# Delta rule on one core: transposed keys in another PSUM bank, scratch of level 0 in a third, output sums one projection step later

## The chip, the cores and the metric

The kernel runs on one core of one Trainium2 chip. The metric is the device time of one execution in microseconds, given as the median of three runs. One further execution was taken with the hardware profiler; all rows below come from it.

## The reference

The reference is a two-layer encoder trunk over 512 tokens of width 1024. Layer 1 has, beside a memory attention, a gated delta rule with 8 heads of width 128. That part is what matters here:

```python
m = where(strict, einsum('bhncd,bhnsd->bhncs', k_beta, k) * decay, 0)
t_inv = triangular_solve(eye + m, eye, lower=True, unit_diagonal=True)
u = t_inv @ v_beta
w = t_inv @ (k_beta * exp(g))
k_dec = k * exp(g_last - g)
def step(state, inp):                 # chunk after chunk
    v_new = u_c - w_c @ state
    o     = qd @ state + a_c @ v_new
    state = state * gl + k_dec^T @ v_new
    return state, o
o = rms_norm(o, out_norm) * silu(z)   # per head, before the output projection
```

The kernel computes it in chunks of 128 tokens, four to a head (`NT = 4`), and inverts `eye + m` level by level: level 0 on single elements, levels 1 to 4 inside 32x32 blocks, level 5 joins 32 to 64, level 6 joins 64 to 128.

## The kernel before

Everything is written out by hand per engine: five instruction streams, each in its own order, held together by semaphores. No planner moves anything. `wait_ge(S.x, n)` holds that engine's whole stream until semaphore `x` has counted to `n`.

Projections are made with fp32 split into two rounded parts, so each 128x128 weight tile costs three matmuls of 512 columns (`product`, L622). A head needs four weight blocks of eight such tiles: queries, keys, values, gate z. These 32 tiles of the **next** head are dealt out between the small matmuls of the delta rule of this head: `fill(first, end)` issues the tiles of that range, and one tile is called a dense portion here. So TensorE has projection work to do while VectorE and ScalarE prepare the next small operand.

The order on TensorE in `delta(h)` (L753) around the change is: two dense portions; the row of decays and betas of the head, broadcast by one matmul (L764) into bank `D[2]`; four transposes of the normalised keys `KN` (L634, from `transposes4`) into `D[5]`; one portion; the Gram matrix of the keys (L772) into `D[1]`; the sums over the squared outputs of the **previous** head (`output_sums`, L730 and L731) into `D[0]`; six portions (3 to 9); the products of keys and queries (L782) into `D[0]`; three portions; then the levels, each with two groups of small matmuls (L797 and L820 for levels 1 to 4, L801, L823 and L827 for level 5, L805 and L830 for level 6). At level 5 a part goes into `D[5]`. The four chunks of the recurrence follow (L845 to L865), which add up the head's output in `D[5]`. The group L797 writes `D[3]`.

`D[5]` therefore holds the outputs of the previous head until VectorE has read them in `o_t1` (L1963, recorded at L1709, inside `stt`). That is why the key transposes wait for `o_t1`.

VectorE's order over the border between two heads is: `normed_k` (the keys times their inverse norm, at L1703, counts `kn_done`), the sum of squares of the outputs (L1960), a copy of the projected z (L1712), `o_t1` (L1709), the decay mask (L1878, reads `D[2]`), `split_o` (L1706, counts `osq_lo`, on which `output_sums` waits), a copy of the values (L1712), the Gram matrix times decays (L1703, after `gg_done` and ScalarE's `dm_done`), level 0 (four quarter multiplies into `D[3]`, a subtraction, and `V.transpose` at L1893, which counts `y_done`), `o_finish` (L1867, after ScalarE's `o_rstd`), and `kdec` (L1897: the transposed keys in PSUM times decays, counts `kdec_done`). The convolution taps of the next head and the levels come behind it.

ScalarE's order is: the exponential of the decay row from `D[2]`, the squares of q, four exponentials of the decay mask (L1427), `o_root` (logarithm and exponential over the output sums, after `oss`), the copy `MM` of the Gram matrix (after `z_pre`, counts `t_done`), then rounding the next weight block (`upper`) and the first tap of the convolution (L1358), and so on.

All elementwise helpers record their own line, so many different instructions share L1248 (ScalarE) and L1703, L1706, L1709, L1712 (VectorE).

Of the kernel before, what the change touches and what calls it, by code (L numbers as in the profile page):

```python
# [23 lines left out]
P = 128  # L24
# [65 lines left out]
QB = P // 4  # L90
(IDENT, ONES, ONES64, TRIU, NEG_LOWER, SMALL) = range(6)
SMALL_IDENT, SMALL_LEVEL0 = 0, 1
# [34 lines left out]
def yoco_kernel(nc, x, mem, w_stream, w_out, w_down, w_ba, cols_in, squares_in, dist_in, out):  # L127
    with ExitStack() as ctx:
# [21 lines left out]
        bank = ctx.enter_context(nc.psum_tensor("bank", [P, 8, 512], F32))  # L150
# [164 lines left out]
        def due(n):  # L315

            return not isinstance(n, int) or n > 0
# [16 lines left out]
        def w(i):  # L334
            return ws[:, i, :]

        def w4(i):
            return ws[:, i, :].rearrange("p (t c) -> p t c", t=NT)

        def sq(i):  # L340
            return sq_c[:, i, :]

        def small(i):

            at = SMALL * P + QB * i
            flat = sq_c[:].rearrange("p a c -> p (a c)")[:, at:at + QB]
            return flat.unsqueeze(1).to_broadcast([P, NT, QB])

        def half_rows(q):
            return slice(HB * q, HB * (q + 1))  # L350

        def quarter(q):
            return slice(QB * q, QB * (q + 1))

        def per_tile(ap):
            return ap.rearrange("p (t c) -> p t c", t=NT)

        def key_block(t, q, c):

            return ws[quarter(q), MM, P * t + QB * c:P * t + QB * (c + 1)]  # L360

        def inverse(t, q):

            return ws[quarter(q), TT, QB * t:QB * (t + 1)]

        def turned(t, q):

            return ws[quarter(q), TT, P + QB * t:P + QB * (t + 1)]

        def masked(t, q):  # L370

            return ws[quarter(q), PM, QB * t:QB * (t + 1)]

        def upper_half(t):

            return ws[half_rows(0), TT, 2 * P + HB * t:2 * P + HB * (t + 1)]
# [12 lines left out]
        def psum(b, n=512):  # L389
            return bank[:, b, 0:n]  # L390

        def psum4(b):
            return bank[:, b, :].rearrange("p (t c) -> p t c", t=NT)

        def tt(i, t):
            return ws[:, i, t * P:(t + 1) * P]
# [4 lines left out]
        D = [2, 3, 4, 5, 6, 7]  # L401
# [11 lines left out]
        NG, GG, _, GL, EDEC, LNB, TMP1, TMP2 = range(8)  # L413

        def dn(i):
            return dn_s[:, i, :].rearrange("p (h t) -> p h t", h=DN_HEADS)

        def dn_bcast(i, h):

            return dn(i)[:, h, :].unsqueeze(2).to_broadcast([P, NT, P])  # L420
# [192 lines left out]
        def _(pe):  # L613
# [18 lines left out]
            def transposes4(dst, source):  # L632
                for t in range(NT):
                    mm = nc.tensor.transpose(bank[:, dst, t * P:(t + 1) * P], tt(source, t), sq(IDENT))  # L634
                return mm
# [105 lines left out]
            def output_sums(h):  # L741

                pe.wait_ge(S.osq_lo, h + 1)
                two_part_sums(D[0], act_lo[:, OHI_T, :], act_lo[:, OLO_T, :]).then_inc(S.oss, 1)
# [8 lines left out]
            def delta(h, fill):  # L753
# [9 lines left out]
                    pe.wait_ge(S.v_done, NT * h)  # L763
                nc.tensor.matmul(psum(D[2]), pick(h), gate_rows, start=True, stop=True).then_inc(S.gb_done, 1)  # L764
                pe.wait_ge(S.kn_done, h + 1)
                if due(h):
                    pe.wait_ge(S.o_t1, h)
                transposes4(D[5], KN).then_inc(S.ktr_done, 1)
                fill(2, 3)

                for t in range(NT):
                    mm = nc.tensor.matmul(bank[:, D[1], t * P:(t + 1) * P], tt(KN, t), tt(KN, t), start=True, stop=True)  # L772
                mm.then_inc(S.gg_done, 1)
                if due(h):
                    output_sums(h - 1)
                fill(3, 9)

                pe.wait_ge(S.c_ready, 2 * h + 1)
                if due(h):
# [5 lines left out]
                for k in range(1, LEVELS):  # L785
                    quarters, join, last = k < LEVELS - 2, k == LEVELS - 2, k == LEVELS - 1
                    if k == 1:
                        pe.wait_ge(S.t_done, h + 1)
                        pe.wait_ge(S.y_done, Y_PER_HEAD * h + 1)
                    else:  # L790
                        pe.wait_ge(S.tz_done, TZ_PER_HEAD * h + k - 1)
                    if last:
                        pe.wait_ge(S.y_done, Y_PER_HEAD * h + LEVELS)
                    for t in range(NT):
                        if quarters:
                            for q in range(4):
                                mm = nc.tensor.matmul(bank[quarter(q), D[3], QB * t:QB * (t + 1)],  # L797
                                                      key_block(t, q, q), inverse(t, q), start=True, stop=True)
                        elif join:
                            for r in range(2):  # L800
                                mm = nc.tensor.matmul(bank[quarter(2 * r + 1), D[3], QB * t:QB * (t + 1)],  # L801
                                                      key_block(t, 2 * r, 2 * r + 1), inverse(t, 2 * r),
                                                      start=True, stop=True)
                        else:
                            mm = nc.tensor.matmul(bank[half_rows(1), D[3], HB * t:HB * (t + 1)],  # L805
                                                  ws[half_rows(0), MM, P * t + HB:P * (t + 1)], upper_half(t),
                                                  start=True, stop=True)
                    mm.then_inc(S.p_mm, 1)
                    fill(10 + 2 * k, 11 + 2 * k)
                    pe.wait_ge(S.p_done, P_PER_HEAD * h + (k if quarters else LEVELS - 1 if join else LEVELS))  # L810
                    pe.wait_ge(S.y_done, Y_PER_HEAD * h + (Y_PER_HEAD - 2 if last else k))
                    if k == 1:
                        pe.wait_ge(S.vb_done, h + 1)
                        pe.wait_ge(S.kdec_done, h + 1)
                    if last:
                        pe.wait_ge(S.tz_done, TZ_PER_HEAD * h + LEVELS - 1)
                    for t in range(NT):
                        if quarters:
                            for q in range(4):
                                mm = nc.tensor.matmul(bank[quarter(q), D[4], QB * t:QB * (t + 1)], turned(t, q),  # L820
                                                      masked(t, q), start=True, stop=True)
                        elif join:
                            nc.tensor.matmul(bank[quarter(1), D[5], QB * t:QB * (t + 1)], turned(t, 1), masked(t, 1),  # L823
                                             start=True, stop=True)
                            for r in range(2):
                                q = 2 * r + 1
                                mm = nc.tensor.matmul(bank[quarter(2 * r), D[4], QB * t:QB * (t + 1)], masked(t, q),  # L827
                                                      turned(t, q), start=True, stop=True)
                        else:
                            mm = nc.tensor.matmul(bank[half_rows(0), D[2], HB * t:HB * (t + 1)],  # L830
                                                  ws[half_rows(1), PM, HB * t:HB * (t + 1)],
                                                  ws[half_rows(1), ZZ, P * t + HB:P * (t + 1)], start=True, stop=True)
                    mm.then_inc(S.tz_mm, 1)
                    fill(11 + 2 * k, 12 + 2 * k)
# [65 lines left out]
            def next_heads(h):  # L900

                def fill(first, end):
                    for j in range(first // KT, (end - 1) // KT + 1):
                        proj_dn(h + 1, j, range(max(first - KT * j, 0), min(end - KT * j, KT)))
                return fill
            each_head(lambda h: delta(h, next_heads(h)))

            def mem_project(layer, j, ks):
# [790 lines left out]
        def _(dve):  # L1699
            V = nc.vector  # L1700

            def mul(out_, x_, y_):
                return V.tensor_tensor(out_, x_, y_, ALU.mult)  # L1703

            def sub(out_, x_, y_):
                return V.tensor_tensor(out_, x_, y_, ALU.subtract)  # L1706
# [169 lines left out]
            def delta(h, fill, following=True):  # L1876
# [8 lines left out]
                mul(psum(D[1]), psum(D[1]), w(DD)).then_inc(S.mt_done, 1)  # L1885
                dve.wait_ge(S.mt_done, h + 1)
                for q in range(4):
                    mul(per_tile(bank[quarter(q), D[3], 0:P]), psum4(D[1])[quarter(q), :, QB * q:QB * (q + 1)],
                        small(SMALL_LEVEL0)[quarter(q)]).then_inc(S.z_pre, 1)
                dve.wait_ge(S.z_pre, 4 * h + 4)  # L1890
                sub(per_tile(w(TT)[:, P:2 * P]), small(SMALL_IDENT), per_tile(psum(D[3], P))).then_inc(S.z_done, 1)
                dve.wait_ge(S.z_done, h + 1)
                V.transpose(w(TT)[:, 0:P], w(TT)[:, P:2 * P]).then_inc(S.y_done, 1)  # L1893
                if due(h):
                    o_finish(h - 1)
                dve.wait_ge(S.ktr_done, h + 1)
                mul(w4(KDEC), psum4(D[5]), dn_bcast(EDEC, h)).then_inc(S.kdec_done, 1)  # L1897
                fill(0, 1)
                for k in range(1, LEVELS):
                    n = (LEVELS - 1) * h + k  # L1900
# [345 lines left out]
```

## Time and profile before

| | |
|---|---|
| median of three runs | 1453.14 us (1451.79 to 1453.53) |
| profiled execution, its own time | 1453.59 us |
| profiled execution, span | 1451.8 us |
| TensorE matmul busy | 1411.7 us, 97% of the span |
| VectorE / ScalarE / GpSimd busy | 546.5 / 576.8 / 560.4 us |
| mean granted TensorE clock | 0.995 of full speed |

The span runs from the first to the last instruction; the time of an execution is some 1.8 us more. Starts are in us from the start of the span. A matmul row's duration is modelled from start to drain and successive matmuls overlap, so distances between starts tell what a matmul costs the stream. An entry in square brackets is idle time of that engine before the row, and what released it.

### The profile page before, as it was taken

How to read it: one execution, taken by the hardware profiler on the slowest of the kernel's cores; microseconds unless marked ns; L12 is line 12 of the kernel's file. 1: busy time of each engine (PE TensorE's matmuls, PEld its weight loads, DVE VectorE, ACT ScalarE, POOL GpSimd, SP SyncE). 2: the span in 40 equal slices, each digit the busy share in tenths (PEclk: the TensorE clock that was granted, in tenths of full speed). 3: DMA queues.
4: the chain of work that ended last, by engine and by line, in shares of the span. 5: the costliest groups of instructions: out<-in, count | busy, mean ns of one | idle time of the engine just before them, and what ended most of it. 6: DMA issues, size and time to landing. Idle time of an engine off the chain costs nothing.

```text
span 1451.8 us, 24193 instructions
## 1 busy us (share of the span) xinstructions
PE 1411.7 (97%) x9320; PEld 1137.8 (78%) x9320; DVE 546.5 (38%) x1052; ACT 576.8 (40%) x985; POOL 560.4 (39%) x276
## 2 busy tenths in 40 slices
PE   5999999999999999999999999999999999999998
PEld 5977777777777888888888887778788888888887
DVE  3545666666644222210122224774322221122210
ACT  5654544554525342322223334875334232223221
POOL 3543233333321444354434443122345344433432
PEclk9999999999999999999999999999999999999999
DMA  6431111111110423233332242111233323422232
GB/s 237 131 105 55 60 59 59 46 57 40 47 54 26 125 93 109 85 91 108 101 101 79 80 125 91 48 49 45 77 109 102 102 69 100 135 84 91 74 95 78
DMA packets 39230, 124.15 MB, mean 86 GB/s; under 512 B 4192, under 2 KB 5472, under 8 KB 39136
## 3 DMA queue, kind: packets, MB, share of 16 engines
q1 hardware_dynamic: 38976, 122.55, 27.1%
q8 instruction: 69, 1.13, 0.3%
q10 hardware_dynamic: 160, 0.26, 0.1%
q14 instruction: 25, 0.20, 0.0%
HBM read 120.44 MB, written 2.10 MB: 84 GB/s over the span
## 4 chain that ended last, share of the span: by engine, by line
PE 90%; DVE 5%; ACT 3%; issue 1%; DMA 0%; DVEq 0%; SPq 0%; ACTq 0%
PE bank L622 78%; DVE ws L1709 2%; ACT ws L1248 1%; PE bank L945 1%; PE bank L820 1%; PE bank L973 1%; DVE ws L1712 1%; ACT L1450 1%; DVE act_lo L1709 1%; PE bank L797 1%; PE bank L1180 1%; PE bank L1204 1%; PE bank L1191 1%; PE bank L962 0%; PE bank L772 0%
## 5 line engine op out<-in xcount | busy, mean ns | idle before, releaser
L558 POOL TENSOR_TENSOR w_lo<-w_raw,w_hi 128x1024 fp32r<-128x1024 f32 (+1 forms) x248 | 529.4, 2150 | 771.2 <-ACT w_hi L1248 771.2
L622 PE MATMUL bank<-act_hi,w_hi 128*128 128x512 f32 (+1 forms) x1776 | 709.6, 400 | 4.0 <-DVE act_lo L1709 2.6
L622 PE MATMUL bank<-act_hi,w_lo 128*128 128x512 f32 (+1 forms) x1776 | 680.0, 383 | 0.0
L622 PE MATMUL bank<-act_lo,w_hi 128*128 128x512 f32 (+1 forms) x1776 | 679.6, 383 | 0.0
L622 PEld LDWEIGHTS bank<-act_hi,w_hi 128*128 128x128 f32 x1776 | 335.0, 189 | 71.1 <-issue 4.9
L622 PEld LDWEIGHTS bank<-act_hi,w_lo 128*128 128x128 f32 x1776 | 334.7, 188 | 65.8
L622 PEld LDWEIGHTS bank<-act_lo,w_hi 128*128 128x128 f32 x1776 | 335.5, 189 | 58.6 <-issue 3.1
L1248 ACT ACTIVATE w_hi<-w_raw 128x1024 fp32r<-128x1024 f32 (+1 forms) x248 | 228.6, 952 | 93.1 <-PE bank L622 91.0
L1703 DVE TENSOR_TENSOR ws<-bank,ws 128x512 f32<-128x512 f32 x110 | 75.9, 691 | 334.5 <-PE bank L622 324.3
L1248 ACT ACTIVATE ws<-ws 128x512 f32<-128x512 f32 (+2 forms) x120 | 79.8, 666 | 165.9 <-DVE ws L1703 112.4
L2044 DVE TENSOR_TENSOR xT<-xT,bank 128x512 f32<-128x512 f32 (+1 forms) x48 | 33.0, 688 | 258.6 <-PE bank L622 258.6
L1248 ACT ACTIVATE act_hi<-ws 128x512 fp32r<-128x512 f32 (+1 forms) x52 | 32.8, 631 | 238.1 <-DVE ws L1703 238.1
L1709 DVE SCALAR_TENSOR_TENSOR ws<-bank,cols,ws 128x510 f32<-128x510 f32 (+3 forms) x80 | 59.0, 738 | 22.4 <-ACT ws L1358 22.0
L1712 DVE COPY ws<-bank 128x512 f32<-128x512 f32 (+5 forms) x103 | 45.2, 439 | 53.7 <-PE bank L622 21.4
L1248 ACT ACTIVATE ws<-xT 128x512 f32<-128x512 f32 (+1 forms) x24 | 15.2, 632 | 107.1 <-DVE xT L2044 107.1
L1358 ACT ACTIVATE ws<-bank,cols 128x512 f32<-128x512 f32 x24 | 16.5, 687 | 101.1 <-PE bank L622 88.3
L1248 ACT ACTIVATE ws<-bank 128x512 f32<-128x512 f32 x49 | 29.1, 594 | 68.0 <-PE bank L1096 44.9
L1706 DVE TENSOR_TENSOR act_lo<-ws,act_hi 128x512 fp32r<-128x512 f32 (+1 forms) x44 | 30.5, 693 | 34.5 <-ACT act_hi L1248 34.5
L1703 DVE TENSOR_TENSOR ws<-ws 128x512 f32<-128x512 f32 x52 | 37.1, 714 | 3.1
L1248 ACT ACTIVATE ws<-bank,cols 128x512 f32<-128x512 f32 (+1 forms) x36 | 22.9, 635 | 29.9 <-PE bank L1104 8.7
L1248 ACT ACTIVATE ws<-ws,st 128x128 f32<-128x128 f32 (+1 forms) x66 | 27.0, 412 | 11.7 <-DVE st L2158 11.7
L1706 DVE TENSOR_TENSOR ws<-ws,bank 128x128 f32<-128x128 f32 x56 | 16.1, 288 | 41.1 <-PE bank L820 32.9
(175 smaller groups left out, 934.4 us busy)
## 6 DMA issues: line engine op xcount, KB each, us to landing
w_raw<-w_stream SPq DMA_DIRECT2D x154, 512.0 KB, 3.3
w_raw<-w_out SPq DMA_DIRECT2D x32, 384.0 KB, 3.1
w_raw<-w_down SPq DMA_DIRECT2D x32, 384.0 KB, 3.1
w_raw<-w_down SPq DMA_DIRECT2D x32, 320.0 KB, 3.3
ws<-x_in SPq DMA_DIRECT2D x1, 2048.0 KB, 8.2
ws<-mem_in SPq DMA_DIRECT2D x2, 512.0 KB, 4.7
out<-ws SPq DMA_DIRECT2D x1, 1024.0 KB, 4.2
out<-ws SPq DMA_DIRECT2D x1, 768.0 KB, 3.6
```

What stands on the lines that cost most here:

```text
L558: nc.gpsimd.tensor_tensor(w_lo[:, s, 0:width * P], w_raw[:, s, 0:width * P], w_hi[:, s, 0:width * P].bitcast(F32), ALU.subtract).then_inc( ...
L622: mm = nc.tensor.matmul(acc, wt[:, c % RING, wsl], at[:, act0(k0 + k), off:off + n], start=(start and k == 0 and m == 0), stop=(stop and k ...
L797: mm = nc.tensor.matmul(bank[quarter(q), D[3], QB * t:QB * (t + 1)], key_block(t, q, q), inverse(t, q), start=True, stop=True)
L820: mm = nc.tensor.matmul(bank[quarter(q), D[4], QB * t:QB * (t + 1)], turned(t, q), masked(t, q), start=True, stop=True)
L945: mm = nc.tensor.matmul(bank[:, D[2] + t // 2, (t % 2) * MEM_LEN:(t % 2 + 1) * MEM_LEN], tt(RAW_Q[layer][j], t), kmem[:, u, :], start=True ...
L1248: return nc.scalar.activation(out_, in_, func, **kw)
L1358: nc.scalar.activation(w(CQ + j), psum(j % 2), ACT.Copy, scale=conv_w(h, j, 3)).then_inc(S.cv_tap, 1)
L1703: return V.tensor_tensor(out_, x_, y_, ALU.mult)
L1706: return V.tensor_tensor(out_, x_, y_, ALU.subtract)
L1709: return V.scalar_tensor_tensor(out=out_, in0=x_, scalar=scalar, in1=y_, op0=op0, op1=op1)
L1712: return V.tensor_copy(out_, x_)
L2044: V.tensor_tensor(xT[:, k, :], xT[:, k, :], psum(j), ALU.add).then_inc(S.acc_free, 1)
```

## The change

The transposed keys go to `D[3]` in place of `D[5]`, and the wait for `o_t1` in front of them goes. `D[3]` was the scratch of level 0, which moves to `D[2]`, the bank of the decay row. Since the first level's matmuls write `D[3]`, the wait for `kdec_done` moves from the second group of level 1 to the first. The first write to `D[5]` is now at level 5, so the wait for `o_t1` stands there. `output_sums` moves behind one more dense portion.

```diff
-                if due(h):
-                    pe.wait_ge(S.o_t1, h)
-                transposes4(D[5], KN).then_inc(S.ktr_done, 1)
+                transposes4(D[3], KN).then_inc(S.ktr_done, 1)
                 fill(2, 3)
...
                 mm.then_inc(S.gg_done, 1)
+                fill(3, 4)
                 if due(h):
                     output_sums(h - 1)
-                fill(3, 9)
+                fill(4, 9)
...
                         pe.wait_ge(S.y_done, Y_PER_HEAD * h + 1)
+                        pe.wait_ge(S.kdec_done, h + 1)
...
                     if k == 1:
                         pe.wait_ge(S.vb_done, h + 1)
-                        pe.wait_ge(S.kdec_done, h + 1)
+                    if join and due(h):
+                        pe.wait_ge(S.o_t1, h)
...
                 for q in range(4):
-                    mul(per_tile(bank[quarter(q), D[3], 0:P]), psum4(D[1])[quarter(q), :, QB * q:QB * (q + 1)],
+                    mul(per_tile(bank[quarter(q), D[2], 0:P]), psum4(D[1])[quarter(q), :, QB * q:QB * (q + 1)],
                         small(SMALL_LEVEL0)[quarter(q)]).then_inc(S.z_pre, 1)
...
-                sub(per_tile(w(TT)[:, P:2 * P]), small(SMALL_IDENT), per_tile(psum(D[3], P))).then_inc(S.z_done, 1)
+                sub(per_tile(w(TT)[:, P:2 * P]), small(SMALL_IDENT), per_tile(psum(D[2], P))).then_inc(S.z_done, 1)
...
-                mul(w4(KDEC), psum4(D[5]), dn_bcast(EDEC, h)).then_inc(S.kdec_done, 1)
+                mul(w4(KDEC), psum4(D[3]), dn_bcast(EDEC, h)).then_inc(S.kdec_done, 1)
```

## Rows read from the trace of the kernel before

**Rows 1.** The page: TensorE's busy time, and the chain that ended last, by engine.
```profile
PE 1411.7 (97%) x9320; PEld 1137.8 (78%) x9320; DVE 546.5 (38%) x1052; ACT 576.8 (40%) x985; POOL 560.4 (39%) x276
PE 90%; DVE 5%; ACT 3%; issue 1%; DMA 0%; DVEq 0%; SPq 0%; ACTq 0%
```

**Rows 2.** Waits of TensorE, whole span: us in total, times, longest us.
```profile
PE bank L642 <- ACT ws L1248: 11.9, 1, 11.9
PE bank L634 <- DVE ws L1709: 9.1, 7, 1.4
```

**Rows 3.** Timeline of TensorE in head 4: start us, us, engine, line.
```profile
267.39 0.40 PE L622 MATMUL bank<-act_hi,w_lo 128*128 128x512 f32 x1
267.71 0.50 PE L764 MATMUL bank<-act_hi 64*128 64x512 f32 x1
269.48 0.63 PE L634 MATMUL bank<-sq_c,ws 128*128 128x128 f32 x4 [1.26 <-DVE ws L1709]
269.86 0.47 PE L622 MATMUL bank<-act_hi,w_hi 128*128 128x512 f32 x1
...
270.63 1.05 PE L772 MATMUL bank<-ws 128*128 128x128 f32 x8
271.44 0.48 PE L730 MATMUL bank<-act_lo 128*128 128x512 f32 x1
271.75 0.39 PE L731 MATMUL bank<-act_lo 128*128 128x512 f32 x1
...
276.09 1.05 PE L782 MATMUL bank<-ws 128*128 128x128 f32 x8
...
279.13 0.45 PE L797 MATMUL bank<-ws 32*32 32x32 f32 x32
```

**Rows 4.** Timeline of VectorE in the same stretch.
```profile
266.67 0.69 DVE L1703 TENSOR_TENSOR ws<-ws,bank 128x512 f32<-128x512 f32 x1 [0.83 <-ACT bank L1248]
...
268.59 0.74 DVE L1709 SCALAR_TENSOR_TENSOR ws<-bank,cols,ws 128x512 f32<-128x512 f32 x1
269.25 0.68 DVE L1878 TENSOR_TENSOR ws<-bank,sq_c 128x512 f32<-128x512 f32 x1
269.85 0.68 DVE L1706 TENSOR_TENSOR act_lo<-bank,act_lo 128x512 fp32r<-128x512 f32 x1
...
271.72 0.70 DVE L1703 TENSOR_TENSOR bank<-bank,ws 128x512 f32<-128x512 f32 x1 [0.60 <-PE bank L772]
...
274.11 0.31 DVE L1893 STREAM_TRANSPOSE ws<-ws 128x128 f32<-128x128 f32 x1
...
274.91 0.68 DVE L1703 TENSOR_TENSOR ws<-bank,dn_s 128x512 f32<-128x512 f32 x1
278.16 0.75 DVE L1709 SCALAR_TENSOR_TENSOR ws<-bank,cols,ws 128x511 f32<-128x511 f32 x1 [2.57 <-ACT ws L1358]
```

**Rows 5.** Timeline of ScalarE in the same stretch.
```profile
270.12 1.28 ACT L1427 ACTIVATE ws<-ws,dn_s 128x128 f32<-128x128 f32 x4 [0.40 <-DVE ws L1878]
272.27 0.69 ACT L1248 ACTIVATE ws<-bank,cols 128x512 f32<-128x512 f32 x1 [0.87 <-PE bank L731]
272.99 0.63 ACT L1248 ACTIVATE ws<-ws 128x512 f32<-128x512 f32 x1
273.78 0.60 ACT L1248 ACTIVATE ws<-bank 128x512 f32<-128x512 f32 x1 [0.16 <-DVE bank L1703]
274.28 1.05 ACT L1248 ACTIVATE w_hi<-w_raw 128x1024 fp32r<-128x1024 f32 x1
277.30 0.69 ACT L1358 ACTIVATE ws<-bank,cols 128x512 f32<-128x512 f32 x1 [1.97 <-PE bank L782]
```

**Rows 6.** Timeline of head 0, which has no wait for `o_t1`.
```profile
112.21 0.50 PE L764 MATMUL bank<-act_hi 64*128 64x512 f32 x1
112.64 0.66 PE L634 MATMUL bank<-sq_c,ws 128*128 128x128 f32 x4
```

**Rows 7.** Timeline of head 1: the decay row, the key transposes and VectorE's `split_o`.
```profile
149.65 0.50 PE L764 MATMUL bank<-act_hi 64*128 64x512 f32 x1
151.52 0.63 PE L634 MATMUL bank<-sq_c,ws 128*128 128x128 f32 x4 [1.37 <-DVE ws L1709]
151.89 0.68 DVE L1706 TENSOR_TENSOR act_lo<-bank,act_lo 128x512 fp32r<-128x512 f32 x1
```

## The prediction

> **What bounds the kernel.** I read the page first. TensorE is busy for 97% of the span and carries 90% of the chain that ended last [rows 1]: the kernel is bound by TensorE's stream, so a change pays where it removes an idle stretch of TensorE or work from it, and nowhere else. This change removes no matmul. So the next view is the waits of TensorE. After one wait for the input at the start (11.9 us, not touched), the largest entry is the key transposes, L634, released by VectorE at L1709: 7 waits, 9.1 us in total, the longest 1.4 us [rows 2]. Seven is the number of heads 1 to 7, in which the wait for `o_t1` exists. Then I read the timelines of the three engines over one head border; all of them repeat each 39.3 us, heads 1 and 7 with a wait of 1.37 us, heads 2 to 6 with 1.26 to 1.29 us.
>
> In head 4 the decay row starts at 267.71 and the transposes only at 269.48 [rows 3]. VectorE runs in one unbroken chain there: `normed_k` ends at 266.67 + 0.69 = 267.36, `o_t1` runs from 268.59 to 269.33, and the transposes start 0.15 us after its end [rows 3, 4]. The keys themselves were there 2.1 us earlier. So the wait is for the bank `D[5]` alone, and the change gives the keys another bank.
>
> **The term that is won.** From the start of the decay row to the start of the transposes the seven heads take 9.1 us of idle time plus 7 x 0.50 us, the modelled length of the decay row's matmul: 12.6 us [rows 2, 3]. Without the wait the transposes follow the decay row as closely as TensorE lets them. Two rows bound that distance. In head 0, without this wait, it is 0.43 us, and there the keys arrived only just before, so it is an upper bound [rows 6]. Going from the dense stream to the decay row (128 rows to 64 rows of the array, also 512 columns ahead of it) costs 0.32 us [rows 3]; I take this as the lower one. I take the middle, 0.38 us. The gain is 12.6 - 7 x 0.38 = 9.9 us; at the two ends 9.6 and 10.4 us.
>
> [...] The last matmul of a dense portion and the decay row stand 0.32 us apart, and head 0 has 0.43 us [rows 3, 6]. [...]
>
> **Is something else late next?** I move TensorE's part of head 4 forward and look at each wait it meets. The transposes start at 267.71 + 0.38 = 268.09, 1.39 us earlier than before.
>
> The keys (`kn_done`) are ready at 267.36 [rows 4]: 0.7 us to spare.
>
> The output sums wait for `split_o`. Before, they started 271.44 - 269.48 = 1.96 us behind the transposes [rows 3]. The change puts one dense portion ahead of them; a portion costs 270.63 - 269.86 = 0.77 us [rows 3]. New start: 268.09 + 1.96 + 0.77 = 270.82. `split_o` ends at 269.85 + 0.68 = 270.53 and nothing ahead of it on VectorE comes from TensorE's moved part [rows 4]; with the 0.15 us that a release took above, 270.68. So 0.14 us to spare. Had the sums stayed in their place they would have been wanted at 270.05, and TensorE would have stood 0.6 us per head: this edit costs nothing and covers that. In head 1 the decay row starts at 149.65, and `split_o` ends at 151.89 + 0.68 = 152.57 [rows 7]; the sums are wanted at 149.65 + 0.38 + 2.73 = 152.76 against 152.72: just in time, and head 7 is the same. The portion itself is only moved (3 to 9 becomes 3 to 4 and 4 to 9): no matmul more or less.
>
> The Gram matrix comes 1.39 us earlier, but VectorE multiplies it only when ScalarE's four exponentials are done too, at 270.12 + 1.28 = 271.40 [rows 5]. So that multiply moves from 271.72 to about 271.46, by 0.26 us [rows 4], and with it level 0, `MM`, the transpose and `kdec`.
>
> ScalarE's `o_root` starts after the sums: 270.82 + 0.31 + 0.39 + 0.13 = 271.65 in place of 272.27 and ends near 273.0 [rows 3, 5]. The copy `MM` then waits for `z_pre` as before (273.5) and is not held by it; nor is `o_finish`.
>
> The keys' products L782 want the logarithm done (272.4); TensorE comes at 276.09 - 1.39 = 274.70. No wait.
>
> The first level starts at 279.13 - 1.39 = 277.74 [rows 3]. It now waits for `kdec_done` too, which ends at 274.91 - 0.26 + 0.68 = 275.33 [rows 4]: 2.4 us to spare. `t_done` (274.1) and `y_done` (274.2) are earlier still [rows 4, 5]. The moved wait therefore costs nothing; what hides it is the dense portions 4 to 12. If that cover were gone, the whole chain of the levels would stand behind it.
>
> Behind that, the convolution's first tap on ScalarE is released by L782 itself (idle 1.97 us before it) and VectorE's taps by ScalarE (idle 2.57 us) [rows 4, 5]; ScalarE is free at 275.1 and L782 ends near 275.7, so these follow TensorE. The rest of the head is tied to TensorE in this way, and comes 1.39 us earlier as a whole, with the short stands of TensorE in it kept. GpSimd and the weight loads are released from the same stream; no row of the waits names either as what holds TensorE.
>
> `o_t1` at level 5 is wanted some 20 us after it is done, and level 0 in `D[2]` is the same VectorE work on another bank; the decay row there has been read by VectorE itself and by ScalarE before. Both cost nothing. The waits that change place are as many as before, and the second one asks for values long reached.
>
> **Sum.** Gain 9.9 us, no term against it. The profiled execution's own time is 1453.59 (span 1451.8), so it would become 1443.7; the median of the runs shown is 1453.14, 0.45 lower, and becomes 1443.2.
>
> **Rivals.**
>
> Forecast, the wait goes and nothing takes its place: 9.6 to 10.4 us, 1442.7 to 1443.5, with the runs' own spread of some 0.9 us around it. Chance 0.72.
>
> The wait moves to the output sums. Against it stands 0.14 us of margin in heads 2 to 6, for it that this is small and in heads 1 and 7 nearly nothing. Each 0.1 us that `split_o` is late costs 7 x 0.1 = 0.7 us. If TensorE arrives first in all heads and loses the overlap of its weight load at the restart too (0.1 to 0.4 us a head), the gain is 7 to 9 us: 1444 to 1446. Chance 0.17.
>
> [...] In rows: the matmuls of a dense portion start 0.23 us apart, and a transposition behind the decay row at that distance would give 12.6 - 1.6 = 11.0 us, if it did not run into `split_o`. But it does: the sums would be wanted at 267.71 + 0.23 + 2.73 = 270.67 against 270.68. So 1442.1. Chance 0.04.
>
> The change does less than it says: some other engine's rhythm sets the border, for instance VectorE's chain from `normed_k` on, so that part of the shift is lost again at the levels, where TensorE already stands for tenths of a us. Then 3 to 7 us are left, 1446 to 1450. Against it: VectorE and ScalarE both sit idle for 2 us between the border and the first tap. Chance 0.05.
>
> On the other side, slower than before: the late output sums hold ScalarE in `o_root`, behind it stand `MM`, and `o_finish` holds VectorE ahead of `kdec`, for which the first level now waits with no group of matmuls between. TensorE would stand at L797. It stands from the moment when `kdec` ends after 277.74, 2.4 us later than worked out above, and the head becomes longer than before only if it ends after 279.13, 3.8 us later. Each us beyond that would cost 7 us: 1 us gives 1460. Nothing in the rows comes near. Chance 0.02.
>
> **Range and chances.** The first two cases and the third hold 0.93; a range from 1441.7 (the third less half the spread) to 1446.5 holds some 8 in 10 and a little more. A difference of 0.2%, 2.9 us, is about what a measurement of this kernel can tell from no change. Faster 0.94, the same 0.04, slower 0.02.
>
> **What the profile after would show.** The entry L634 released by L1709 gone from TensorE's waits; decay row to transposes 0.32 to 0.43 us in heads 1 to 7; one head in 37.9 us where it was 39.3; no idle before L730, or tenths at most; none before L797; VectorE's Gram multiply released by ScalarE's L1427 instead of L772; `kdec` done over 2 us ahead of L797. The prediction is wrong if an idle stretch appears ahead of L730 or L797, or if the head's length falls by less than the distance at the transposes does.

## The result, and the profile after

The changed kernel takes 1444.61 us (median of five runs, 1443.19 to 1444.78) against 1453.14 us before, also five runs: ratio 0.9941, 95% interval 0.9926 to 0.9955, that is 8.6 us less with an interval of 6.5 to 10.8. Run again beside other kernels it took 1444.37 us against 1453.81, ratio 0.9942 (0.9929 to 0.9956). The forecast was 1443.2 with a range of 1441.7 to 1446.5.

The page of the changed kernel, first the span, then busy time, then the chain that ended last by engine:

```profile
span 1442.8 us, 24178 instructions
PE 1412.0 (98%) x9320; PEld 1139.5 (79%) x9320; DVE 547.2 (38%) x1052; ACT 576.7 (40%) x985; POOL 560.5 (39%) x276
PE 93%; DVE 3%; ACT 2%; issue 1%; DMA 0%; DVEq 0%; SPq 0%; ACTq 0%
```

The same work is done in 9.0 us less span: busy time is what it was, and three hundredths of the chain moved from VectorE and ScalarE to TensorE, because the way round over `o_t1` is no longer part of it [rows 1]. The waits of TensorE in the changed kernel, longest first (us in total, times, longest):

```profile
PE bank L642 <- ACT ws L1249: 11.8, 1, 11.8
PE bank L622 <- DVE act_lo L1710: 2.7, 1, 2.7
PE bank L1151 <- ACT ws L1249: 2.3, 1, 2.3
```

The entry of 9.1 us at L634 [rows 2] is gone, and no entry at L730 or L797 took its place. TensorE's timeline in head 4, the stretch of [rows 3] (the Gram matrix is now at L770, the products of keys and queries at L781):

```profile
265.30 0.40 PE L622 MATMUL bank<-act_hi,w_lo 128*128 128x512 f32 x1
265.63 0.50 PE L764 MATMUL bank<-act_hi 64*128 64x512 f32 x1
266.06 0.66 PE L634 MATMUL bank<-sq_c,ws 128*128 128x128 f32 x4
266.47 0.47 PE L622 MATMUL bank<-act_hi,w_hi 128*128 128x512 f32 x1
...
267.25 1.05 PE L770 MATMUL bank<-ws 128*128 128x128 f32 x8
...
268.60 0.40 PE L622 MATMUL bank<-act_hi,w_lo 128*128 128x512 f32 x1
268.83 0.40 PE L730 MATMUL bank<-act_lo 128*128 128x512 f32 x1
...
272.72 1.05 PE L781 MATMUL bank<-ws 128*128 128x128 f32 x8
...
275.76 0.45 PE L797 MATMUL bank<-ws 32*32 32x32 f32 x32
```

The transposes follow the decay row by 0.43 us; before it was 1.77 us [rows 3]. The sums L730 follow the last matmul of the portion ahead of them by 0.23 us, the pace of the dense stream: they wait for nothing. From one decay row to the next it is 38.0 us in heads 2 to 5 where it was 39.3. VectorE in the same stretch, to be laid beside [rows 4]:

```profile
264.60 0.69 DVE L1704 TENSOR_TENSOR ws<-ws,bank 128x512 f32<-128x512 f32 x1 [0.84 <-ACT bank L1249]
...
267.78 0.68 DVE L1707 TENSOR_TENSOR act_lo<-bank,act_lo 128x512 fp32r<-128x512 f32 x1
...
269.47 0.70 DVE L1704 TENSOR_TENSOR bank<-bank,ws 128x512 f32<-128x512 f32 x1 [0.41 <-ACT ws L1428]
...
272.67 0.68 DVE L1704 TENSOR_TENSOR ws<-bank,dn_s 128x512 f32<-128x512 f32 x1
274.79 0.75 DVE L1710 SCALAR_TENSOR_TENSOR ws<-bank,cols,ws 128x511 f32<-128x511 f32 x1 [1.45 <-ACT ws L1359]
```

`split_o` ends at 268.46, 0.37 us ahead of L730. The Gram multiply at 269.47 is now released by ScalarE's exponentials, no longer by TensorE. `kdec` ends at 273.35, 2.4 us ahead of L797. VectorE's idle time before the first tap fell from 2.57 to 1.45 us, and that before the Gram multiply from 0.60 to 0.41: together 1.31 us, which is where the time that TensorE won was taken from. There is still some left. ScalarE, beside [rows 5]:

```profile
269.58 0.69 ACT L1249 ACTIVATE ws<-bank,cols 128x512 f32<-128x512 f32 x1 [0.24 <-PE bank L731]
270.30 0.63 ACT L1249 ACTIVATE ws<-ws 128x512 f32<-128x512 f32 x1
271.54 0.60 ACT L1249 ACTIVATE ws<-bank 128x512 f32<-128x512 f32 x1 [0.61 <-DVE bank L1704]
```

`o_root` waits 0.24 us for the sums and ends 0.6 us before the copy `MM` can start, so the later sums hold nothing behind it.

### The profile page after: what moved, and what is told of

Read it like the earlier page. It is cut to its first block, busy times and chain, and to the rows that moved or that the text cites. A ratio compares the mean times of both kernels' runs of the same rounds, so it can differ in the third digit from the quotient of the medians.

```text
span 1442.8 us, 24178 instructions
## 1 busy us (share of the span) xinstructions
PE 1412.0 (98%) x9320; PEld 1139.5 (79%) x9320; DVE 547.2 (38%) x1052; ACT 576.7 (40%) x985; POOL 560.5 (39%) x276
## 4 chain that ended last, share of the span: by engine, by line
PE 93%; DVE 3%; ACT 2%; issue 1%; DMA 0%; DVEq 0%; SPq 0%; ACTq 0%
PE bank L622 80%; ACT ws L1249 1%; PE bank L946 1%; PE bank L821 1%; PE bank L974 1%; DVE ws L1710 1%; DVE act_lo L1710 1%; PE bank L797 1%; PE bank L1181 1%; PE bank L634 1%; PE bank L1205 1%; PE bank L1192 1%; DVE ws L1713 1%; PE bank L963 1%; PE bank L781 0%
```

## The experiments

### The sums in their old place

```diff
                 mm.then_inc(S.gg_done, 1)
-                fill(3, 4)
                 if due(h):
                     output_sums(h - 1)
-                fill(4, 9)
+                fill(3, 9)
```

> The changed kernel with the output sums back in their old place, six dense portions behind them. Theory one (the wait moves from the bank to the sum of squares): the sums are wanted 1.31 us earlier than in the kernel before, at 270.13 in its head 4, but VectorE's split_o lets them go only near 270.68; TensorE stands 0.4 to 0.6 us in front of L730 in seven heads, the gain over the kernel before is 0.65 to 0.76 us a head, some 5 us in all: 1448. Rival: the place of the sums has no effect, no idle time at L730, 1444.6 like the changed kernel.

1447.91 us (five runs), ratio to the kernel before 0.9956 (0.9943 to 0.9970). TensorE's waits, then TensorE and VectorE's `split_o` in head 4:

```profile
PE bank L730 <- DVE act_lo L1706: 1.6, 7, 0.3
```

```profile
268.90 1.05 PE L770 MATMUL bank<-ws 128*128 128x128 f32 x8
270.14 0.50 PE L730 MATMUL bank<-act_lo 128*128 128x512 f32 x1 [0.20 <-DVE act_lo L1706]
```

```profile
269.41 0.68 DVE L1706 TENSOR_TENSOR act_lo<-bank,act_lo 128x512 fp32r<-128x512 f32 x1
```

Before, L730 followed the Gram matrix by 0.81 us [rows 3]; here by 1.24 us, so TensorE stands 0.43 us, at the low end of what was expected. The idle column shows only 0.20 us of it, because it counts from the modelled end of the last matmul, not from when the next could start. The sums start 0.05 us after `split_o` ends (269.41 + 0.68 = 270.09), not the 0.15 us that the prediction took over from the release of the transposes. Decay row to decay row is 38.5 us in heads 2 to 5, 0.45 us more than in the changed kernel, and 0.58 and 0.49 us more in heads 1 and 6; with head 7 that makes 3.4 us. The medians differ by 3.3 us, but these are of two comparisons; by their ratios to the kernel before it is 2.2 us, and the two intervals overlap. The later sums are therefore worth some 3 us of the gain, by the traces more surely than by the run times, and only together with the removed wait, as the next two kernels show.

### The wait put back

```diff
+                if due(h):
+                    pe.wait_ge(S.o_t1, h)
                 transposes4(D[3], KN).then_inc(S.ktr_done, 1)
```

> The changed kernel with the wait for o_t1 put back ahead of the key transposes, which still write D[3]; all else stays as changed. Theory one (the wait is all that was won): 7 waits at L634 of 1.26 to 1.37 us return and the time is that of the kernel before, 1453. Rival: the other bank, or the later sums, saves something of its own, then the time is clearly below, by 2 us or more.

1453.23 us (eleven runs), ratio 0.9999 (0.9990 to 1.0008). The wait is back as it was:

```profile
PE bank L634 <- DVE ws L1712: 9.2, 7, 1.4
```

With the other banks, the moved `kdec` wait and the later sums all in, but this wait too, nothing is won. So the gain needs the wait gone, and the other banks bring nothing of their own.

### Only the sums moved

```diff
-                fill(3, 9)
+                fill(4, 9)
```

(with `fill(3, 4)` ahead of `output_sums`, in the kernel before)

> The kernel before with only the output sums moved one dense portion later, the keys still in D[5] behind the wait. Theory one (the sums never held TensorE there): no change, 1453, within 0.1%. Rival: the later sums hold ScalarE's logarithm and behind it the copy MM and the first level, slower by tenths of a us a head, 1455.

1453.68 us (eleven runs), ratio 1.0001 (0.9992 to 1.0010). The wait at L634 is 9.2 us as ever. So while the wait is there, the place of the sums has no price, either way.

### Six more multiplications ahead of `kdec`

```diff
+                for i in range(6):
+                    if i or due(h):
+                        dve.wait_ge(S.spare_done, 6 * h + i)
+                    mul(per_tile(spare[:]), psum4(D[3]), dn_bcast(EDEC, h)).then_inc(S.spare_done, 1)
                 mul(w4(KDEC), psum4(D[3]), dn_bcast(EDEC, h)).then_inc(S.kdec_done, 1)
```

> The changed kernel with six more multiplications of the size of kdec put ahead of it on VectorE in every head (work added, nothing left out). It measures the slack of the moved wait: in the changed kernel's head 4 kdec ends at 273.35 and L797 starts at 275.76, 2.4 us later. Six more at 0.6 to 0.7 us take 3.6 to 4.2 us, so L797 is expected to stand 1.2 to 2.0 us in each of 8 heads, released by VectorE: 10 to 16 us more than the changed kernel, 1454 to 1460. Rival: the slack is larger or the work is hidden elsewhere, under 5 us more.

1466.01 us (four runs), ratio 1.0089 (1.0073 to 1.0104), 21.4 us above the changed kernel, where 10 to 16 were expected. The waits, and VectorE and TensorE in head 3 (L799 is the L797 of the changed kernel, L766 its L764):

```profile
PE bank L799 <- DVE ws L1706: 14.2, 8, 2.0
```

```profile
241.26 4.30 DVE L1706 TENSOR_TENSOR spare<-bank,dn_s 128x512 f32<-128x512 f32 x6
...
245.48 0.68 DVE L1706 TENSOR_TENSOR ws<-bank,dn_s 128x512 f32<-128x512 f32 x1
...
246.31 0.45 PE L799 MATMUL bank<-ws 32*32 32x32 f32 x32 [1.87 <-DVE ws L1706]
```

Against the decay row, `kdec` ends 4.2 us later than in the changed kernel and L799 starts 1.9 us later, which leaves 2.3 us of slack: the 2.4 us worked out, less the 0.15 us from the end of `kdec` to L799. The rival that would have made the kernel slower is thus real as a mechanism; it only lies 2.3 us away. The stands came out as expected: L799 starts 1.3 us later in head 0 and 1.75 to 2.05 us later in the others, 14.7 us in all. The rest of the 21.4 us was not expected. Head 3 takes 39.98 us from decay row to decay row, 1.93 more than the 38.05 of the changed kernel; others take 41.4 and one 42.5. What they have and head 3 hasn't is shown by the windows around 205 us, in head 2 (busy us of each engine and count, granted clock, DMA share, GB/s):

```profile
200.00:205.00 5.00, 3.10 (x44) 2.08 (x42) 4.46 (x8) 2.15 (x3) 3.53 (x2) 0.99 0.00 0
205.00:210.00 5.00, 5.00 (x103) 3.21 (x102) 1.55 (x4) 0.00 (x0) 2.40 (x2) 0.50 0.58 191
210.00:215.00 5.00, 5.00 (x115) 3.24 (x108) 3.05 (x8) 3.14 (x4) 0.00 (x0) 0.82 0.07 22
```

After the stand at L799 (TensorE busy for 3.10 us of the first five) TensorE runs at half its clock for a while: the granted clock is 0.50 from 205 to 210 us, where it was 0.99 in the window ahead. Four of heads 0 to 6 have such a stretch and are longer by 1.5, 2.6, 1.4 and 1.4 us on top of the stand; head 7 has one too, worth 2.8 us by the start of its level 5. Against these 9.7 us, this execution has no such stretch near 50 and near 880 us, where that of the changed kernel has one each. In the kernel before, stands of 1.3 us were followed by none between 105 and 400 us. The six multiplications could be blamed in place of the stands; the next kernel, with two of them and no stand, has no such stretch there either, though it does not test six without a stand.

### Two more multiplications ahead of `kdec`

The same edit with two in place of six.

> The changed kernel with two more multiplications of the size of kdec ahead of it in every head, where six made TensorE stand 1.9 us at L797. Two take 1.4 us, kdec then ends 1.0 us before L797 wants it: no stand at L797 and the time of the changed kernel, 1444.6. If the slack of 2.4 us is wrong, or if kdec_plus6 lost its time by VectorE's work itself and not by the stand, some us more.

1442.50 us (five runs), ratio 0.9929 (0.9916 to 0.9943), against 0.9942 (0.9929 to 0.9956) for the changed kernel in the same comparison: the intervals overlap by half. VectorE in head 4:

```profile
270.56 1.41 DVE L1706 TENSOR_TENSOR spare<-bank,dn_s 128x512 f32<-128x512 f32 x2
271.88 0.68 DVE L1706 TENSOR_TENSOR ws<-bank,dn_s 128x512 f32<-128x512 f32 x1
272.67 0.75 DVE L1712 SCALAR_TENSOR_TENSOR ws<-bank,cols,ws 128x511 f32<-128x511 f32 x1
```

The idle time before the first tap is filled, and TensorE does not notice: a head takes 38.0 us, so the 1.9 us between the medians are no effect of the edit. The 1.4 us of work added on VectorE cost nothing; the 4.3 us of the six multiplications reached L797.

### A portion between decay row and transposes

```diff
-                transposes4(D[3], KN).then_inc(S.ktr_done, 1)
                 fill(2, 3)
+                transposes4(D[3], KN).then_inc(S.ktr_done, 1)
```

> The changed kernel with the dense portion put between the decay row and the key transposes, in place of behind them. It asks why the transposes come 0.43 us after the decay row where 0.38 was forecast. Theory one (going from 64 to 128 rows of the array costs it, whatever comes next): the dense portion then starts 0.43 us after the decay row, and the time is the same, 1444.6. Rival (it belongs to the transposes): the portion starts after 0.23 to 0.32 us and 8 heads save 0.1 to 0.2 us each, near 1443.4.

1442.95 us (five runs), ratio 0.9926 (0.9913 to 0.9940); a head takes 38.06 us, 0.05 more than in the changed kernel of the same comparison, so the 1.4 us by which the median is lower are no effect of the order. The decay row and what follows it:

```profile
265.91 0.49 PE L764 MATMUL bank<-act_hi 64*128 64x512 f32 x1
266.33 0.50 PE L622 MATMUL bank<-act_hi,w_hi 128*128 128x512 f32 x1
266.67 0.40 PE L622 MATMUL bank<-act_lo,w_hi 128*128 128x512 f32 x1
```

The portion too starts 0.42 us behind the decay row. The distance belongs to the decay row's matmul, on 64 rows of the array with one on 128 rows behind it, and not to the transposes. Whether it is the change in rows that costs it was not tried by itself.

### The convolution's taps one level earlier

```diff
                 fill(0, 1)
+                fill(0, 2)
...
-                    if k <= 2:
-                        fill(0, k + 1)
+                    if k == 1:
+                        fill(0, 3)
+                    elif k == 2:
+                        pass
```

> The changed kernel with the second and third convolution tap of the queries each one level earlier on VectorE, so that the accumulator of the third projection block is free sooner. In the changed kernel the dense portion of level 3 starts 0.60 us after its group L797, where the other levels have 0.38. Theory one (VectorE's late tap holds it): the distance becomes 0.38 and 8 heads save 0.22 us each, 1.8 us, 1442.9. Rival: VectorE gets later at level 1 by as much and the stand only moves to L821, no gain.

1443.12 us (five runs) beside 1444.37 for the changed kernel on the same chip; ratios 0.9931 (0.9918 to 0.9945) and 0.9942 (0.9929 to 0.9956). By the medians 1.25 us, less than a measurement of this kernel can tell. The trace can: TensorE at level 3 of head 4, where the changed kernel has 0.60 us from the start of the group to the start of the portion,

```profile
280.85 0.45 PE L797 MATMUL bank<-ws 32*32 32x32 f32 x32
281.45 0.50 PE L622 MATMUL bank<-act_hi,w_hi 128*128 128x512 f32 x1
```

and this one

```profile
277.74 0.45 PE L797 MATMUL bank<-ws 32*32 32x32 f32 x32
278.13 0.50 PE L622 MATMUL bank<-act_hi,w_hi 128*128 128x512 f32 x1
```

has 0.39, and a head takes 37.82 us in place of 38.01 in the changed kernel of the same comparison. From the first decay row to the last it is 1.26 us less. Head 7 saves nothing: its distance there was 0.38 us already in the changed kernel, which the expectation of eight heads and 1.8 us had overlooked. By the heads' length it is the shortest version here; by the run times that is not shown.

## Why the prediction was right

**The step that carried it**, that the seven waits are for the bank and not for the keys, holds: the wait alone, put back, takes the whole gain away, and the later sums alone bring nothing.

**The size.** 9.9 us were forecast, 8.6 (6.5 to 10.8) measured. In the traces heads 2 to 5 became 1.29 us shorter each, not 1.39, and heads 1, 6 and 7 (this one up to its level 5) 1.36 to 1.41; that is 9.3 us for seven, inside the measured interval (the repeat won 9.4 by its medians). The term that was a little off is the distance from decay row to transposes: I took 0.38 us, between 0.32 and 0.43, and it is 0.42 or 0.43 in every head. Head 0 had shown it already, and the late keys that I blamed for it had no part in it, since the others have it with keys long ready. That is 0.35 us in all. Most of the rest is the transposes themselves, a term that the sum did not have: they occupy the stream for 0.41 us where, right behind a stand, they occupied it for 0.38 (also in the kernel with the wait put back, so it is not the bank). The third rival, 1442.1, took the 0.23 us between the matmuls of a dense portion for this distance. That spacing is there in the changed kernel too (268.60 to 268.83 in head 4), but behind the decay row no run shows it: the smallest distance in any trace is 0.42 us.

**From 9.3 to the spans' 9.0.** From the first decay row to the last it is 273.37 us before and 265.41 after (265.28 in the repeat), 7.96 less, for the six waits of heads 1 to 6. Behind the last decay row it is 2.97 less: 1.4 for the wait of head 7, and some 1.5 because the execution of before ran at half clock once near 425 us and that of the changed kernel did not. Ahead of the first decay row it is 1.93 more (114.14 against 112.21; 111.86 in the repeat): there the execution of the changed kernel had a half-clock stretch near 50 us, and 1.15 of the 1.93 us arise from there on. The other 0.78 us stay unexplained; the half-clock stretch near 20 us in the execution of before would have told the other way. The five traces with the stretch near 50 us reach the first decay row at 113.3 to 114.3 us, the five without it at 111.6 to 112.2. The edit touches none of these parts. The rows, three of before and one of the changed kernel:

```profile
15.00:20.00 5.00, 2.35 (x14) 2.02 (x13) 3.00 (x10) 4.69 (x11) 1.50 (x1) 0.86 0.55 198
20.00:25.00 5.00, 5.00 (x36) 5.00 (x36) 0.42 (x1) 0.76 (x3) 3.22 (x2) 0.79 0.47 130
425.00:430.00 5.00, 5.00 (x14) 3.43 (x15) 1.63 (x3) 2.57 (x4) 0.90 (x1) 0.68 0.00 0
```

```profile
50.00:55.00 5.00, 4.48 (x25) 4.48 (x26) 4.74 (x8) 4.90 (x13) 0.00 (x0) 0.66 0.08 33
```

**The sums.** Forecast was a start at 3.11 us behind the decay row; it is 3.20. The kernel with the sums in their old place shows when `split_o` lets them go: at 2.87 us, and 2.98 in heads 1 and 7. So the margin is 0.33 us, and 0.22 in heads 1 and 7, where 0.14 and 0.04 were worked out, and the rival "the wait moves to the sums" did not come true by that much. Both errors fell on the right side: TensorE came 0.09 us later, and the release took 0.05 us and not 0.15. With a margin this small that was partly luck. Without the moved portion the rival would have come true: the stand was priced at 0.6 us a head and is 0.43, with 0.45 to 0.58 on the head's length. The 0.1 to 0.4 us more that this rival put on a lost overlap of the weight load no run shows: in heads 2 to 5 TensorE stands 0.43 us and the head is 0.43 to 0.48 us longer, which leaves at most 0.05 us for it.

**`kdec`, `MM`, `o_root`.** All three came within 0.1 us of the computed places behind the decay row: 2.4 us to spare at L797 (confirmed by six multiplications that ate it and two that didn't), the Gram multiply handed from TensorE's release to ScalarE's, `o_root` not in anyone's way.

**The rival that other engines set the rhythm** and the shift would be lost again at the levels did not come true: in head 4, 1.34 us are won at the start of the transposes, 1.30 at the Gram matrix, 1.29 at the first level and 1.30 at the end of the head. By the letter of its own sign the prediction would be wrong, because the head's length did fall by less than the distance at the transposes; but the 0.04 us are lost at the transposes and the portion behind them, not at the levels.

## What to carry to other kernels

When an engine waits, ask first whether for data or for a place. Here the keys were ready 2.1 us before the transposes, and with another bank all of the wait went; the scratch of VectorE that gave way cost nothing. Then move the engine's stream forward on paper and look what it meets next: the next wait would have cost 0.4 us a head, and one portion of independent work in front of it was worth some 3 us, though by itself it is worth nothing. And read distances from start to start: the idle column showed 0.20 us of the stand of 0.43 us at the sums.

## What the runs showed of the hardware

- The decay row's matmul, 512 columns on 64 rows of the array, was followed by one on 128 rows after 0.42 to 0.44 us wherever the transposes did not wait for `o_t1`, in all ten traces, whether that was a transposition or a dense matmul (0.42 to 0.43 us) and with all semaphores long reached. Within a dense portion it was 0.23 us in most places, and from the dense stream into the decay row 0.32 to 0.33 us.
- From the end of a VectorE instruction to the start of the matmul that it released it was 0.14 to 0.15 us at the transposes in the kernel before and at L799 with six multiplications, and 0.05 us at L730 with the sums in their old place.
- TensorE at half clock was seen in short stretches in every profiled execution: taken in windows of one microsecond, the granted clock is 0.50 from 19 to 22 and from 425 to 428 us in that of before and from 51 to 54 us in one of the changed kernel, and 1.00 shortly before and after each. Each of those near 20, 50 and 425 us takes 1.6 to 1.8 us of full-speed time: the granted clock is 0.66 to 0.68 where one lies in a single five-microsecond window, and shared out where it lies in two. Where they lie differs between executions: near 50 us in one of the changed kernel and near 20 us in the other, and behind the same matmul near 425 us in that of before and near 414 us in that with the taps early, there in no other; one is near 880 to 890 us in all but the kernel with six multiplications, and one in the last microseconds of every execution. Apart from the one at the end, they lie right behind a stand of TensorE, of 2.65, 2.10, 0.84 and 2.3 us in this order, but the same stands are there in executions that keep the full clock: after the 2.10 us near 50 us the granted clock is 0.66 in one execution of the changed kernel and 1.00 in the other. One stretch more or less is as much as the spread of the run times, 1443.2 to 1444.8 us. With six multiplications, stands of 1.75 to 2.05 us a head were followed by such stretches in five of seven heads; in the kernel before, stands of 1.26 to 1.37 us by the idle column were followed by none; what exactly brings one about was not tried.
